# A fused four-block kernel on one core: norm constants ahead, a modulation inside the first token merge, later transform matrices, attention with filler matmuls and banks of its own, branches reordered

## The reference

```python
x = x + rms_norm(u @ w_out[l], norm_post[l]) * gate        # after every mixer; the context too, where it is still needed
h = rms_norm(x, g_pre) * (1 + scale) + shift               # shift, scale, gate = silu(c) @ w_mod[n] + b_mod[n]
# Hyena: filters from a small sine network, times a window, then in the frequency domain
y = irfft(rfft(v) * rfft(k)) + v * skip
# token layer: three branches from h @ w_in
ret  = retention(rq, rk, rv);  o_ret  = rms_norm(ret) * silu(rg)
diff = (softmax(q1 k1) - lam * softmax(q2 k2)) @ dv;  o_diff = rms_norm(diff) * (1 - lam0) * silu(dg)
o_mlp = mu * (w_s @ layer_norm(mv) + b_s) * silu(mg)
y = sum(sigmoid(logits_b) * (o_b @ w_bo[b]) for the three b) @ w_o
```

## Time and profile before

| | before |
|---|---|
| median of 3 runs | 2841.23 us |
| the profiled execution | 2839.73 us |
| its span, first to last instruction | 2837.9 us |
| mean granted TensorE clock | 0.983 |
| PE busy | 2703.7 us (95%) |
| DVE, ACT, POOL busy | 1019.2, 691.0, 404.6 us |
| memory read | 251.71 MB, 89 GB/s over the span |

### The profile page before, as it was taken

One profiled execution on the slowest core, in us unless ns is written; L12 is line 12 of the kernel. 1 busy time (PEld: TensorE's weight loads), 2 busy tenths in 40 slices (PEclk: granted clock), 3 DMA queues, 4 the chain that ended last, 5 costly groups with the idle time before them and its releaser, 6 DMA issues.

```text
span 2837.9 us, 66946 instructions
## 1 busy us (share of the span) xinstructions
PE 2703.7 (95%) x29910; PEld 1891.1 (67%) x29910; DVE 1019.2 (36%) x2256; ACT 691.0 (24%) x1461; POOL 404.6 (14%) x429
## 2 busy tenths in 40 slices
PE   5999999999999997899999989999899999999898
PEld 1677777777777776558878764445544457684687
DVE  3644454554444454332334023110631113320512
ACT  3334333433333332011121021001610003101401
POOL 2433333333333331000001000000000000000000
PEclk8999999999999999899999999999999999999999
DMA  6211111111111111733433732222022264342143
GB/s 235 73 35 40 37 42 42 35 35 35 35 44 35 35 40 47 247 111 129 152 110 99 282 112 74 74 68 65 8 82 74 75 235 165 109 136 74 46 155 97
DMA packets 81780, 257.07 MB, mean 91 GB/s; under 512 B 11575, under 2 KB 19352, under 8 KB 80792
## 3 DMA queue, kind: packets, MB, share of 16 engines
q1 hardware_dynamic: 74560, 239.71, 25.6%
q10 hardware_dynamic: 6328, 9.93, 1.1%
q0 software_dynamic: 608, 3.15, 0.3%
HBM read 251.71 MB, written 1.05 MB: 89 GB/s over the span
## 4 chain that ended last, share of the span: by engine, by line
PE 55%; DVE 3%; DMA 1%; issue 1%; ACT 1%; ACTq 0%; DVEq 0%
PE ps L1804 13%; PE ps L1946 9%; PE ps L1749 8%; PE ps L1683 6%; PE ps L1838 5%; PE ps L1957 4%; PE ps L1656 1%; PE ps L1782 1%; PE ps L1770 1%; DMA sq<-in_window 1%; PE ps L1734 1%; DVE rstd L2588 1%; PE ps L1704 1%; PE ps L1863 1%; PE ps L1858 1%
## 5 line engine op out<-in xcount | busy, mean ns | idle before, releaser
L1804 PE MATMUL ps<-h,ring 128*128 128x256 f32 (+1 forms) x1152 | 370.1, 481 | 16.6 <-issue 16.6
L1804 PEld LDWEIGHTS ps<-h,ring 128*128 128x128 f32 x1152 | 223.3, 194 | 151.6 <-issue 132.6
L1946 PE MATMUL ps<-h,ring 128*128 128x512 f32 (+1 forms) x768 | 255.7, 486 | 0.9 <-ACT general L2177 0.9
L1749 PE MATMUL ps<-h,ring 128*128 128x256 f32 x1024 | 225.2, 379 | 0.8 <-DVE general L2422 0.8
L1749 PEld LDWEIGHTS ps<-h,ring 128*128 128x128 f32 x1024 | 193.9, 190 | 34.4 <-issue 6.2
L1946 PEld LDWEIGHTS ps<-h,ring 128*128 128x128 f32 x768 | 145.6, 190 | 101.9 <-issue 92.1
L1838 PE MATMUL ps<-ring,h 128*128 128x512 f32 x352 | 151.4, 592 | 0.0
L554 PE MATMUL ps<-ring,general 128*128 128x128 f32 x1024 | 150.7, 284 | 0.3 <-DVE general L1228 0.3
L984 ACT ACTIVATE general<-ps 128x256 f32<-128x256 f32 (+1 forms) x192 | 82.1, 427 | 247.1 <-PE ps L695 246.3
L1957 PE MATMUL ps<-general,ring 128*128 128x512 f32 (+1 forms) x384 | 134.4, 496 | 7.1 <-issue 7.1
L535 PE MATMUL ps<-general,ring 128*128 128x512 f32 x256 | 133.1, 606 | 0.8 <-issue 0.8
(11 more groups left out here) (328 smaller groups left out, 4168.5 us busy)
## 6 DMA issues: line engine op xcount, KB each, us to landing
ring<-in_w_mods SPq DMA_DIRECT2D x96, 512.0 KB, 5.2
ring<-in_w_feature SPq DMA_DIRECT2D x72, 512.0 KB, 3.5
ring<-in_w_rkvg SPq DMA_DIRECT2D x64, 512.0 KB, 3.7
ring<-in_w_in SPq DMA_DIRECT2D x48, 512.0 KB, 3.5
ring<-in_w_merge SPq DMA_DIRECT2D x48, 512.0 KB, 3.5
ring<-in_w_out SPq DMA_DIRECT2D x32, 512.0 KB, 4.9
ring<-in_w_token SPq DMA_DIRECT2D x24, 512.0 KB, 3.8
ring<-in_w_merge SPq DMA_DIRECT2D x48, 256.0 KB, 2.7
```

What stands on the lines that cost most here:

```text
L1749: mm = pe.matmul(ps[:, n % 4, 0:NX], weights(key, k), R.h[:, k, 0:NX], start=(k == 0), stop=(k == KD - 1))
L1804: mm = pe.matmul(ps[:, j % 4, 0:width], weights(("feature", l, j), k), R.h[:, k, cols], start=(k == 0), stop=(k == KD - 1))
L1946: mm = pe.matmul(ps[:, 2 * b, 0:NQ], weights(key, k), R.h[:, k, 0:NQ], start=(k == 0), stop=(k == KD - 1))
```

## The change

The plan of the loads and the programs of all five engines change together:

- PE runs modulation 1's steps 0 and 1 in the first part, around `turn_out(KE - 1)`; step m + 1 is done in turn m of the output pass from then on. Modulation 2 likewise runs a step ahead. SP loads the five small filter tensors (`f_w1`, `f_w23`, `f_vec`, `z_t`, `f_w4`) in the first part, ahead of the ring's first loads and behind two waits of its own; ACT loads `dft`, the window, `idft` and the Hyena vectors after its first square. `filters()` waits for the window and `dft` only at its fourth item.
- The loop of pass 0 takes (0,1,1,1,3,2,2,2) filter items, 7 follow it, and the rest comes after the state sums. ACT copies out 15 of the 16 transforms, between its squares and shifts.
- `added`: ACT multiplies each tile by the gain right after its square (`o_gain`). DVE then multiplies by the reciprocal root and adds for rows 0, 1, 3, 4, 6, POOL does both for rows 2, 5, 7.
- In pass 1 the context's state sums come two to a turn, and its root, `scaled` and `shift` one pass turn before the end.
- GAP = 5: five C tiles, three of them ahead of the state sums and two behind.
- The MLP's value tiles (four in layer 0, two in layer 1) leave the values stage. Attention issues two of their matmuls ahead of each job, into banks 4 and 5; the scores have two pairs of banks and not three; ACT copies a tile out every fourth job, and DVE takes its statistics in the loop.
- The retention heads are squared on ACT at the end of retention. The merge sums four heads, makes a logit tile, the spatial matmuls, a logit tile, four head sums, the third logit tile. The square root with its reciprocal becomes a logarithm and an exponential. Each branch matmul waits for its own branch.
- Modulation 3's eight steps move from pass 2 into the eight rounds of layer 0's merge.

The core of the diff:

```diff
+            sp.wait_ge(s["v_done"], KE)
+            sp.wait_ge(s["g_done"], KE)
+            f1, f23, fb, zt = filter_constants(R.G)
+            w4 = carve(R.G, KE * NX, [("w4", (2, E))])["w4"]
+            for dst, src in ((f1[0:33, :], I["f_w1"]), (f23[0:64, :, :], I["f_w23"]), (fb[0:64, :], I["f_vec"]), (zt[0:33, :], I["z_t"]),
+                             (w4[0:64, :, :], I["f_w4"])):
+                sp.dma_start(dst, src).then_inc(S.early, 16)
             for g in range(RING):
                 if g < 4:
                     sp.wait_ge((s["k_done"], s["v_done"], s["r_done"], s["g_done"])[g], KE)
...
             pass
+    modulation_step(pe, R, S, 1, 0)
     pe.wait_ge(s["coef_out"], KE)
     turn_out(KE - 1)
+    modulation_step(pe, R, S, 1, 1)
...
-GAP = 4
+GAP = 5
+GAP_FIRST = 3
+DVE_ROWS, POOL_ROWS = (0, 1, 3, 4, 6), (2, 5, 7)
+FILTER_ITEMS = (0, 1, 1, 1, 3, 2, 2, 2)
...
 
+    modulation(1, 0)
     for m in range(KD):
-        modulation(1, m)
+        if m + 1 < KD:
...
+                modulation(3, m)
         for side in ((X_HALF,) if l else (C_HALF, X_HALF)):
             for m in range(KD):
-                if l == 0 and side == C_HALF:
-                    modulation(3, m)
                 S.add(("last", l, side, m), w_last[m])
...
+def modulation_step(pe, R, S, n, step):
+
+    piece = step % 4
+    for q in range(3):
+        S.landed(pe, ("mod", n, step, q))
+    for k in (2 * piece, 2 * piece + 1):
+        for q in range(3):
+            a = (k % 2) * 512
+            mm = pe.matmul(R.ps[32 * q:32 * q + 4, mod_bank(n), :], R.cond[:, k, :], S.slot(("mod", n, step, q))[:, a:a + 512],
+                           start=(k == 0), stop=(k == KD - 1), tile_position=(0, 32 * q))
+            if k % 2:
+                mm.then_inc(S.used, 1)
+
...
+            if n == 2:
+                pe.wait_ge(s["s_out"], 1)
+            elif n > 2:
+                pe.wait_ge(s["s_act"], n - 2)
...
+    def mlp_values(l):
+
+        y = layer[l]
+        T = mlp_tiles(l)
+        for t in range(T):
+            if t >= 2:
+                pe.wait_ge(y["mv_out"], t - 1)
+            for k in range(KD):
+                key = ("token", l, 2, k // 2)
+                if t == 0 and k % 2 == 0:
+                    S.landed(pe, key)
+                mm = pe.matmul(ps[:, 4 + t % 2, :], R.h[:, k, t * P:(t + 1) * P], weights(key, k % 2, 512), start=(k == 0), stop=(k == KD - 1))
+                if t == T - 1 and k % 2:
+                    mm.then_inc(S.used, 1)
+                elif k == KD - 1:
+                    mm.then_inc(y["mv_done"], 1)
+                yield
+
...
@@ -1905,32 +1957,41 @@
         scores(0)
         scores(1)
         for n in range(J):
+            next(pieces)
+            next(pieces)
+            if n:
+                outputs(n - 1)
             if n + 2 < J:
                 scores(n + 2)
-            if n:
-                outputs(n - 1)
             turn(n)
         outputs(J - 1)
 
...
-        for n in range(2 * HEADS):
+        for n in range(first, first + HEADS):
+            i = n + first
             pe.wait_ge(y["squared"], n + 1)
-            if n >= len(BRANCH_BANKS):
-                pe.wait_ge(y["log"], n - len(BRANCH_BANKS) + 1)
-            pe.matmul(ps[:, branch_bank(n), 0:NQ], R.ones[:, :], R.sq[:, n, 0:NQ], start=True, stop=True).then_inc(y["summed"], 1)
-        yield
+            if i == 2:
+                pe.wait_ge(y["mv_out"], mlp_tiles(l))
+            if i == 8:
+                pe.wait_ge(y["log"], 4)
+            if i > 8:
+                pe.wait_ge(y["mlp_part"], 2 * (i - 9) + 1)
+            pe.matmul(ps[:, branch_bank(i), 0:NQ], R.ones[:, :], R.sq[:, n, 0:NQ], start=True, stop=True).then_inc(y["summed"], 1)
...
     def merge(l):
         y = layer[l]
-        part = branches(l)
+        pe.wait_ge(y["d_out"], len(diff_jobs(l)))
+        pe.wait_ge(y["expd"], 2 * len(diff_jobs(l)))
+        branch_sums(l, 0)
         logits(l, 0, 0)
-        next(part)
+        spatial(l)
         logits(l, 0, 1)
-        next(part)
+        branch_sums(l, HEADS)
         logits(l, 0, 2)
-        pe.wait_ge(y["branch"], 8)
-        pe.wait_ge(y["mlp_out"], 4)
         for b in range(3):
             branch(l, 0, b)
-        for m in range(1, KD):
-            for b in range(3):
-                logits(l, m, b)
-                branch(l, m, b)
+        for m in range(KD):
+            if m:
+                for b in range(3):
+                    logits(l, m, b)
+                    branch(l, m, b)
+            if l == 0:
+                modulation(3, m)
+                if m == 4:
+                    modulation_turn(3, 0)
 
     filt = filters()
     for m in range(KD):
-        modulation(1, m)
+        if 1 <= m < KD - 1:
...
-        for j in range(GAP):
+        for j in range(GAP_FIRST):
             feature(l, j, j == 0)
         for k in range(KD):
             state_sum(2 + 2 * l, k)
+        for j in range(GAP_FIRST, GAP):
+            feature(l, j, False)
...
         act.activation(W.squares[t][:, m, HALF[side]], R.h[:, m, HALF[side]], ACT.Square).then_inc(s["o_sq"], 1)
+        act.wait_ge(s["o_sq"], 8 * p + m + 1)
+        act.wait_ge(s["gain_out"], p + 1)
+        act.activation(R.h[:, m, HALF[side]], R.h[:, m, HALF[side]], ACT.Copy, scale=W.gain_out[:, m:m + 1]).then_inc(s["o_gain"], 1)
...
+    def filter_out(n):
+        f, ch = n // 4, n % 4
+        act.wait_ge(s["s_done"], n + 1)
+        act.activation(W.Kf[:, f, ch * 512:(ch + 1) * 512], ps[:, (3, 7)[n % 2], :], ACT.Copy).then_inc(s["s_act"], 1)
...
+        act.activation(W.moments[:, 0:T, 1], W.moments[:, 0:T, 1], ACT.Ln, bias=R.eps[:, 0:1]).then_inc(y["root"], 1)
+        act.wait_ge(y["root"], 1)
+        act.activation(W.moments[:, 0:T, 1], W.moments[:, 0:T, 1], ACT.Exp, scale=-0.5).then_inc(y["root"], 1)
+
+        def roots(first):
+            for n in range(first, first + HEADS):
+                act.wait_ge(y["summed"], n + 1)
+                act.activation(R.sq[:, n, 0:NQ], ps[:, branch_bank(n + first), 0:NQ], ACT.Ln, bias=R.eps[:, 0:1], scale=1.0 / P).then_inc(y["log"], 1)
+            for n in range(first, first + HEADS):
+                act.wait_ge(y["log"], n + 1)
+                act.activation(R.sq[:, n, 0:NQ], R.sq[:, n, 0:NQ], ACT.Exp, scale=-0.5).then_inc(y["rstd"], 1)
+
+        roots(0)
+        act.wait_ge(y["d_out"], len(diff_jobs(l)))
+        for h in range(HEADS):
+            act.activation(R.sq[:, HEADS + h, 0:NQ], W.F[:, 4 * DQ + h, 0:NQ], ACT.Square).then_inc(y["squared"], 1)
+        roots(HEADS)
 
     def sigmoids(l):
         y = layer[l]
...
         out_square(1, m)
+        if m == 5:
+            state_root(1)
         if m == 6:
-            state_root(1)
+            for k in range(KD):
+                shift(1, k)
...
-        add_odd(p, KD - 1)
+        part = lambda n: (R.h[:, DVE_ROWS[n], HALF[side]], R.x[:, DVE_ROWS[n], HALF[side]])
+
+        def finish_row(n):
+            h, x = part(n)
+            dve.wait_ge(s["x_part"], 5 * p + n + 1)
+            dve.tensor_tensor(x, x, h, ALU.add).then_inc(s["x_dve"], 1)
+
+        dve.wait_ge(s["o_rstd"], p + 1)
+        dve.wait_ge(s["o_gain"], 8 * p + 8)
+        for n in range(5):
+            h, x = part(n)
+            dve.tensor_tensor(h, h, R.rstd[:, HALF[side]], ALU.mult).then_inc(s["x_part"], 1)
+            if n:
+                finish_row(n - 1)
+        finish_row(4)
```

316 lines of the change are left out of this document (162 added, 154 removed).

## The result

| | before | after |
|---|---|---|
| median | 2840.12 us (2838.32 to 2846.41, 4 runs) | 2773.28 us (2771.79 to 2775.64, 4 runs) |
| the profiled execution | 2839.73 us | 2772.66 us |
| its span | 2837.9 us | 2770.8 us |
| mean granted TensorE clock | 0.983 | 0.994 |

The ratio is 0.9762, with a 95% interval of 0.9745 to 0.9779. The forecast was 2763, the range 2743 to 2782. Between the two profiled executions the gain is 67.1 us, where the sum said 78.0.

What follows compares the result with a forecast made beforehand. PE, busy for 95% of the span, was taken as the bound. Gains of 81.5 us less 3.5 for seams left 78.0 off 2839.7, so 2761.7 profiled; the median being 1.5 above, the forecast was 2763 us, range 2743 to 2782.

Steps and rivals of the forecast that it cites:

- A: First output pass and filters: gain 25.0 us, from modulation steps covered in the first part and waits removed.
- Rival 2: Memory bounds the first output pass, which loses 10 us: 2773 us, chance 0.08.
- B: Second output pass: 0 us, since state sums and modulation are moved, not removed.
- C: Features of layer 0: gain 16.0 us, from waits covered and the cold clock's cost gone.
- F: Features of layer 1: gain 7.5 us, from a wait of 5.83 us and slow records covered.
- D: Values, attention and merge of layer 0: gain 17.5 us, with PE the bound at 13.7 us a head.
- E: Modulation 3 moved into layer 0's merge: gain 3.2 us, from a covered 1.58 us wait and eight seams gone.
- G: Layer 1's attention and merge: gain 12.8 us, with a job at 3.84 us.
- H: Adding back at the very end, shared by DVE and POOL: loss 0.5 us, the sums taking 6.9 us.
- Seams: About seven new seams between stages, half a us each: 3.5 us taken off the sum of gains.
- Rival 1: Attention stays bound by the chain and the fillers add to it: gain 60 us, 2781 us, chance 0.11.
- Rivals 3 and 4: 3: stalls only move, 2835 us, chance 0.02; 4: small waits hold PE at 1.2 GHz in rebuilt stages, slower, chance 0.03.

Runs made afterwards that it cites:

- the second profile: The changed kernel, without an edit, profiled once more: 2774.65 us.

## Why the prediction was right, and where its sum was wrong

- **A, forecast 25.0, measured 16.3.** Three terms failed. "I charge them nothing", of SP's early loads: some 4 us of the first part's 5.4 us of lateness; the rest is within what two executions differ by. The two steps, for which I had allowed, did not wait for them; it was PE's other work in the first part that came late. "I leave 1.6" for ACT's copies: the waits in and behind the transforms are 2.42 + 0.69 = 3.1, since ACT's first square, which stands ahead of its first copy, waits for rows that DVE and POOL make at 0.86 each; with DVE alone the 2.42 is 0.31. And a wait that I did not see: the modulation's turn moved from the pass's fourth tile to its third, where DVE still has 5.8 us of sums to do (1.56, with 0.28 for the sine). About 0.5 of the pass's 3.9 stays unassigned. Right were the window, the square, the cold modulation, and the covered step (4.1 at the entry, for 3.5). Rival 2, memory, did not come about: no wait for `ring` in this pass. But its price was 2773, what was measured, so the time alone could not have told it from a forecast that was 10 us short; the waits do.
- **B, 0; measured -1.0.** PE waits 0.91 us once for a modulation slot, which it did not before. ACT's second operation a tile is hidden: the 0.53 behind a pass's last tile is DVE's copy and ACT's square, and stands in the kernel before too (behind its last two passes).

```profile
1558.68 1.89 PE L1659 MATMUL ps<-ring,cond 128*4 128x512 f32 x12 [0.91 <-DMA ring<-in_w_mods]
```

- **C and F, 16.0 and 7.5; measured 16.0 and 7.6.** No wait, no slow clock; the run with GAP 4 confirms the length of the chain.
- **D, 17.5; measured 16.0.** PE is the bound, as forecast, but a head takes 14.84 and not 13.7: I had PE's own work at 6.3 a head, and it is 14.84 - 4 x 1.72 = 7.96. A job of 512 keys takes 0.98 us for outputs, 1.06 for scores and 0.49 for transposes where I booked 0.86, 0.86 and 0.4. The trace before had it: in a job of layer 1 scores take 1.05 from their start to that of the outputs (2639.63 to 2640.68). I had booked columns and not read the rows. From first scores to merge the gain is 45.5 + 27.5 - 61.6 = 11.3 by the unrounded values, for 12.7. The merge gave 4.7, for 4.8.
- **E, 3.2; measured 1.1.** That the eight seams "go" was wrong: a seam costs the 0.2 that I had estimated, but in the merge as well. The wait of 1.58 went, but the waits for ACT's squares grew from 0.56 and 0.53 to 0.53, 1.02 and 0.53, so 0.6 of the 1.6 was left. Some 0.5 of the gain has no place.
- **G, 12.8; measured 12.3.** A job takes 4.26 and not 3.84, for the same reason as in D, which costs 2.1 over the five jobs between the first transposes and the last scores. The last jobs, which have no scores left, give 0.9 of it back, the start 0.4, and the merge 6.2 where I had 6.0.
- **H, -0.5; measured -1.2.** The sums take 6.6 us as before (6.9 forecast). Not foreseen were the stores: the last row to be ready is now 6, and row 7's store stands behind it on SP, so the end comes 3.4 us after the last sum and not 2.3.
- **Seams, -3.5.** A reserve without a place, and it was used: the parts were 14.4 us short in all, the total 10.9.

Rival 1 fell: the fillers fill, they do not add (heads 14.84 us apart, not 16.7, and DVE busy for 29.22 of 44 us). Rivals 3 and 4 fell as well: little of what was removed came back, and from the first dense tile to the last the granted clock is 1.00 in the profile after. Each left a trace, though: the early loads, which rival 3 named, cost the 4 us of A, and in the second profile the clock did fall once, behind the wait of 2.43 us.

Of the signs that the prediction named, one of the wrong ones came: PE waits for ACT among the transforms ahead of Hyena for 2.42 us, and the bound was 1. Of the right ones, the pace of heads and jobs (13.7 and 3.8) was missed by 1.1 and 0.5 us.

## What to carry to other kernels

A transfer moved to a quiet time is not free for the stage it lands in: spread it, and look at that stage's waits without a releaser before and after. When fillers cover a wait, the order of what stands between them may only be right with them; take both out together when you test. Of two engines that exclude each other, giving work to the second gains nothing, as far as these runs show, and the chains that start from the first row become longer.

## What was unexpected of the hardware

- PE's side of the first part lost 4.3 to 8.0 us between 1085 and 1130 us, with memory traffic of 246 GB/s over 13 us ahead of and in them, though it waited for no data: its waits for nothing shown went from 0.35 and 1.44 to 2.30 and 1.95 us, and each such wait ended 1.2 to 1.9 us after a 16 KB packet of the instruction queue had landed.
- Small matmuls cost more than their columns: eight records of outputs 0.98 us, the tail included, against 0.86 by the rate of 512-column records.
- Behind a wait of 2.57 us PE's clock stayed at 2.4 GHz in both layers, while before, behind 5.0 and 5.8 us, it fell to 1.2; it also fell behind 2.15 and 0.89 us close together (the kernel without fillers), behind 1.97 us (adding back all on DVE), and behind 2.43 us in two of nine profiles that have this same wait ahead of the same transforms (2.42 to 2.44 us). So the length of one wait does not tell it here.
